# Meta keys of four attention items in one transpose, index dot products on two row halves, one triangle for the forget sums

## What is computed

```python
# A: forgetting attention, 8 heads of 64
log_f = log_sigmoid(fa + b_forget)
log_f_cum = cumsum(log_f, axis=1)                        # forget sums, (tokens, 8)
s = q @ k.T * scale + f_q - f_k; p = softmax(masked s); o = p @ v
# B: sparse attention, 8 heads; an indexer of 4 heads of 64 picks 64 keys for each query
dots   = einsum('bqhd,bkd->bhqk', q_idx, k_idx)          # 4 index heads, one set of index keys
iscore = einsum('bqh,bhqk->bqk', idx_w, relu(dots)) * 64 ** -0.5
top_score, top_idx = top_k(iscore, 64)
# attention over the chosen keys, then the two branches gated, merged and projected
# mixture of experts: for each expert rows @ w_gate_up[e], clamped SwiGLU, @ w_down[e]
```

## Time and profile before

| | |
|---|---|
| median of 3 runs | 1165.92 us (1164.47 to 4083.46) |
| profiled execution | 1165.41 us, its span 1163.6 us |
| granted PE clock, mean | 0.989 of full speed |
| busy share | PE 95%, PE weight loads 45%, DVE 29%, ACT 18%, POOL 1% |
| DMA | 433.66 MB, mean 373 GB/s |

### The profile page before, as it was taken

One profiled execution on the slowest core, in us unless ns is written; L12 is line 12 of the kernel. 1 busy time (PEld: TensorE's weight loads), 2 busy tenths in 40 slices (PEclk: granted clock), 3 DMA queues, 4 the chain that ended last, 5 costly groups with the idle time before them and its releaser, 6 DMA issues. The chain is left out here.

```text
span 1163.6 us, 13610 instructions
## 1 busy us (share of the span) xinstructions
PE 1101.5 (95%) x5490; PEld 526.2 (45%) x5490; DVE 332.2 (29%) x774; ACT 203.7 (18%) x359; POOL 14.2 (1%) x27
## 2 busy tenths in 40 slices
PE   8999999999999989898989998989999999899997
PEld 6878888554343434343434343433333333343433
DVE  2256443132323131313131313131313131313223
ACT  2438781031101010101010101010101010101012
POOL 3010000000000000000000000000000000000000
PEclk9999999999999999999989999999999999999999
DMA  9814237869999999999999999999999999999994
GB/s 309 278 36 128 90 110 291 359 223 423 422 433 431 431 433 430 431 433 430 433 431 432 431 432 430 433 431 431 433 430 433 430 431 433 431 431 431 426 426 164
DMA packets 39750, 433.66 MB, mean 373 GB/s; under 512 B 3160, under 2 KB 19698, under 8 KB 23204
## 3 DMA queue, kind: packets, MB, share of 16 engines
q1 hardware_dynamic: 38160, 429.45, 88.1%
q0 software_dynamic: 960, 2.30, 0.6%
q10 hardware_dynamic: 596, 1.45, 0.4%
HBM read 432.13 MB, written 1.05 MB: 372 GB/s over the span
## 5 line engine op out<-in xcount | busy, mean ns | idle before, releaser
L1738 PE MATMUL psum<-arena 128*64 128x512 f32 x1016 | 224.4, 595 | 11.0 <-DMA arena<-in_w_gate_up 10.9
L1738 PE MATMUL psum<-ring,arena 128*64 128x512 f32 x968 | 217.4, 604 | 9.2 <-DMA ring<-in_w_gate_up 9.2
L1738 PEld LDWEIGHTS psum<-arena 128*64 128x64 f32 x1016 | 70.9, 137 | 156.8 <-issue 139.9
L1754 PE MATMUL psum<-ring,arena 128*64 128x512 f32 x544 | 123.7, 608 | 15.5 <-DMA ring<-in_w_down 9.1
L1738 PEld LDWEIGHTS psum<-ring,arena 128*64 128x64 f32 x968 | 68.2, 139 | 151.1 <-issue 148.8
L1196 DVE TENSOR_TENSOR arena<-psum,biasT 128x512 f32<-128x512 f32 x64 | 44.3, 692 | 292.3 <-PE psum L1710 288.0
L859 DVE TENSOR_TENSOR arena<-psum,vT 128x512 f32<-128x512 f32 (+1 forms) x42 | 28.4, 681 | 341.7 <-PE psum L1637 331.8
L1754 PE MATMUL psum<-arena 128*64 128x512 f32 x480 | 108.0, 603 | 10.4 <-DMA arena<-in_w_down 10.4
L773 ACT ACTIVATE arena<-psum 128x1024 f32<-128x1024 f32 x32 | 32.7, 1023 | 325.1 <-PE psum L1738 311.7
L1754 PEld LDWEIGHTS psum<-ring,arena 128*64 128x64 f32 x544 | 42.2, 140 | 85.5 <-issue 85.5
L1220 DVE TENSOR_TENSOR h<-h,psum 128x1024 f32<-128x1024 f32 x64 | 75.3, 1218 | 16.0 <-PE psum L1779 14.0
(11 more groups left out here) (233 smaller groups left out, 762.2 us busy)
## 6 DMA issues: line engine op xcount, KB each, us to landing
arena<-in_w_gate_up SPq DMA_DIRECT2D x28, 4096.0 KB, 30.2
ring<-in_w_gate_up SPq DMA_DIRECT2D x27, 4096.0 KB, 30.0
arena<-in_w_down SPq DMA_DIRECT2D x14, 4096.0 KB, 30.1
ring<-in_w_down SPq DMA_DIRECT2D x12, 4096.0 KB, 30.1
ring<-in_w_in SPq DMA_DIRECT2D x14, 1024.0 KB, 12.5
arena<-in_w_gate_up SPq DMA_DIRECT2D x13, 1024.0 KB, 15.9
arena<-in_w_gate_up SPq DMA_DIRECT2D x5, 2048.0 KB, 25.2
ring<-in_w_down SPq DMA_DIRECT2D x10, 1024.0 KB, 16.4
```

Of the source, the lines that this page charges most:

```text
L1738: ins = mm(bank[home + n][h * CAP:(h + 1) * CAP, :], xg[:, c, e * CAP:(e + 1) * CAP], w[:, h * D + n * 512:h * D + (n + 1) * 512], start=c ...
L1754: ins = mm(bank[1][n * CAP:(n + 1) * CAP, :], act[:, c * CAP:(c + 1) * CAP], w[:, n * 512:(n + 1) * 512], start=first, stop=last)
```

## The change

Three edits, all in the mixer:

- **Forget sums.** `ltri` is a strict triangle; the sum had one product with `ltri` and one with the identity for each tile. Now DVE adds the two matrices once (`tri`, in a buffer that is free until the attention loop), and each tile has one product. PE waits for `s_tri`.
- **Index heads.** Two heads' index queries (2 x 64 columns) are transposed together, so that odd heads land in rows 64 to 127. The index keys are copied into both halves of the rows (two DVE copies, `s_kiT`). The products of heads h and h + 1 are issued one after the other on different row halves, into different banks.
- **Meta keys.** DVE writes the 16 meta columns of item k, multiplied, into columns 32 (k % 4) of a buffer `prm` (two halves of 128 columns), with an instruction of its own, then the remaining columns as before. For every fourth item PE transposes the 128 columns of `prm` at once into the bank of that item, and DVE copies the four strips out, ahead of the item's own copy. The other three items have no meta transpose and no meta copy.

```diff
-        qiT = late[:, 0:IH * SEQ].rearrange("p (h k) -> p h k", h=IH)
+        qiT = late[:, 0:IH * SEQ // 2].rearrange("p (h k) -> p h k", h=IH // 2)
...
-        pT = take(4 * 384)
+        pT = take(2 * 640)
+        prm = take(2 * P)
...
+        tri = pT[0][:, 0:P]
...
-                copy_out(("qiT", t), qiT[0:ID, :, t * P:(t + 1) * P],
-                         job_bank(("qiT", t))[0:ID, :].rearrange("p (h k) -> p h k", h=IH))
+                copy_out(("qiT", t), qiT[:, :, t * P:(t + 1) * P],
+                         job_bank(("qiT", t))[:, 0:IH // 2 * P].rearrange("p (h k) -> p h k", h=IH // 2))
...
             dve.wait_ge(s_kst, 16)
+            v.tensor_tensor(tri, ltri, ident, ALU.add).then_inc(s_tri, 1)
...
-            v.tensor_copy(kiT[0:ID, :], job_bank(("kkT", 0))[0:ID, 0:KEYS])
+            for n in range(2):
+                v.tensor_copy(kiT[n * ID:(n + 1) * ID, :], job_bank(("kkT", 0))[0:ID, 0:KEYS]).then_inc(s_kiT, 1)
...
-                    v.tensor_scalar(pr[:, k % 3, 0:w], pr[:, k % 3, 0:w], rk[:, 32 + k:33 + k], None,
+                    heads_meta = slice(k % 8 * 32, k % 8 * 32 + META)
+                    v.tensor_scalar(prm[:, heads_meta], pr[:, k % 3, 0:META], rk[:, 32 + k:33 + k], None, ALU.mult)
+                    v.tensor_scalar(pr[:, k % 3, META:w], pr[:, k % 3, META:w], rk[:, 32 + k:33 + k], None,
                                     ALU.mult).then_inc(s_pn, 1)
...
-                    v.tensor_copy(dst[0:META, 384 + t * P:384 + (t + 1) * P], src[0:META, 256:384])
+                    if k % 4 == 3:
+                        for m in range(4):
+                            v.tensor_copy(pT[2 * (pair % 2) + m // 2][0:META, 384 + m % 2 * P:384 + (m % 2 + 1) * P],
+                                          src[32 * m:32 * m + META, 256:384])
                     empty_end(v.tensor_copy(dst[:, t * P:t * P + (t + 1) * P], src[:, 0:(t + 1) * P]), ("PT", k))
...
             pe.wait_ge(s_logf, 1)
+            pe.wait_ge(s_tri, 1)
...
-                terms = [(lf[0:rows, t, :], ltri[0:rows, 0:rows]), (lf[0:rows, t, :], ident[0:rows, 0:rows])]
+                terms = [(lf[0:rows, t, :], tri[0:rows, 0:rows])]
...
-                for h in range(IH):
-                    ins = tr(job_bank(name)[0:ID, h * P:(h + 1) * P],
-                             qtok[:, t, 768 + h * ID:768 + (h + 1) * ID], ident)
+                for h in range(IH // 2):
+                    ins = tr(job_bank(name)[:, h * P:(h + 1) * P],
+                             qtok[:, t, 768 + 2 * h * ID:768 + 2 * (h + 1) * ID], ident)
                 fill_end(ins, name)
+            pe.wait_ge(s_kiT, 2)
             wait_emptied(pe, ("kkT", 0))
...
-                for h in range(IH):
-                    name = ("dots", t, h)
-                    fill_begin(pe, name)
-                    fill_end(mm(job_bank(name)[:, 0:WIDTH[t]], qiT[0:ID, h, t * P:(t + 1) * P],
-                                kiT[0:ID, 0:WIDTH[t]], start=True, stop=True), name)
+                for h in range(0, IH, 2):
+                    for u in range(2):
+                        fill_begin(pe, ("dots", t, h + u))
+                    for u in range(2):
+                        name = ("dots", t, h + u)
+                        part = slice(u * ID, (u + 1) * ID)
+                        fill_end(mm(job_bank(name)[:, 0:WIDTH[t]], qiT[part, h // 2, t * P:(t + 1) * P],
+                                    kiT[part, 0:WIDTH[t]], start=True, stop=True), name)
...
-                    tr(job_bank(name)[:, k * P:(k + 1) * P], pr[:, i % 3, META + k * P:META + (k + 1) * P],
-                       ident)
-                fill_end(tr(job_bank(name)[0:META, 256:384], pr[:, i % 3, 0:META], ident), name)
+                    ins = tr(job_bank(name)[:, k * P:(k + 1) * P],
+                             pr[:, i % 3, META + k * P:META + (k + 1) * P], ident)
+                if i % 4 == 3:
+                    ins = tr(job_bank(name)[:, 256:384], prm[:, i // 4 % 2 * P:(i // 4 % 2 + 1) * P], ident)
+                fill_end(ins, name)
```

More of the change, by code:

```diff
@@ L320, in build @@
         s_nf = sem("forget_row_beside_keys")
+        s_tri = sem("inclusive_triangle_ready")
+        s_kiT = sem("index_keys_in_both_halves")
         s_kk = sem("index_and_rope_keys_ready")
```

## The result

| | before | after |
|---|---|---|
| median | 1164.88 us (18 runs, 1163.60 to 1166.12 but for one of 4083.46) | 1167.62 us (18 runs, 1166.10 to 1169.01) |
| ratio | | 1.0021, 95% interval 1.0014 to 1.0027 |
| profiled execution, its span | 1165.41, 1163.6 us | 1167.12, 1165.3 us |

The account below looks back on a forecast made before the run. PE bounds the front up to the first expert load at 184.55 us, DMA the rest. Terms -0.49 - 0.20 + 0.135 - 1.4 = -1.95 us took 1165.41 to 1163.5 us; range 1160.7 to 1166.6 us.

Parts of the forecast that it names:

- What bounds the kernel: Whole kernel: PE-bound front of 251 us, DMA-bound rest of 906 us; time off PE's way to 184.55 us moves the end equally.
- Part 1: Forget sums: one triangle removes 6 of 18 PE passes, 0.49 us less on PE.
- Part 2: Index queries and dot products: 0.20 us less from ACT's shorter copy; faster dot products count zero, covered by DVE's selection.
- The term for ACT's copy: Index queries, first tile: ACT's copy takes 0.38 us instead of 0.58, so 0.20 us go.
- The fourth rival: Index dot products: the two row halves run in series, still 1163.5 us; counted within the forecast's 0.55.
- Part 3, the saving: Attention loop: 32 meta transposes become 8, 2.6 us less on PE; about 0.1 us lost at the last transpose.
- Part 3, the multiplication: Second DVE multiplication by 1/sum, 16 meta columns: +0.135 us per item, on the path at the first item.
- Part 3, the copies: End of each four items: four meta copies at 0.20 us steps, +0.60; values 0.14 us late, seven places costing 1.14 us.
- My own sign of being wrong: Values in the attention loop: the prediction is wrong if they wait for over 0.4 us.
- the three other places: Three of the loop's seven waits before the values: slack 0.655 us instead of 0.71, so 0.195 us late each.
- the third: End of each four items: DVE's burst becomes the bound, 0.73 us at each of seven places, 1167.4 us; chance 0.15.

Follow-up runs that it names:

- e6: e3 with the index heads as in the kernel before, one head per transpose and products one by one: 1161.70 us, ratio 0.9977 to the kernel before.
- e7: e3 with six rounds of DVE's selection instead of eight for each tile, so 48 keys picked instead of 64: 1160.48 us, one run.
- e8: e6 with six rounds of DVE's selection instead of eight for each tile, so 48 keys picked instead of 64: 1160.10 us, one run.
- e3: Changed kernel, but the fourth item's main copy comes first with its own signal, the four meta strips after it: 1163.14 us, ratio 0.9981 to the kernel before.
- e4: Changed kernel with all four strip copies reading rows 0 to 15, which alters the attention's meta part: 1164.58 us, ratio 0.9997 to the kernel before.
- e5: Changed kernel with ACT's copies of finished pairs of heads two loop steps later: 1167.07 us, ratio 1.0013 to the kernel before.
- e2: Kernel before with the meta-key part alone: 1167.50 us, ratio 1.0020 to the kernel before.
- e9: Kernel before with the index part alone, two heads on two row halves: 1164.65 us, ratio 0.9993 to the kernel before.
- e10: Kernel before with the forget part alone, one triangle for the sums: 1164.55 us, ratio 0.9997 to the kernel before.
- e11: e3 with the second tile's selection spread over the attention loop's DVE steps: 1159.54 us, ratio 0.9950 to the kernel before.
- e1: Changed kernel with meta keys handled as before, so forget and index parts only: 1164.20 us, ratio 0.9991 to the kernel before.
- e12: e6 with the second tile's selection spread over the attention loop's DVE steps: 1161.42 us, ratio 0.9967 to the kernel before.

## Why the prediction was wrong, step by step

- **What bounds the kernel**: right. PE's way to the first expert load sets the end; the last stage kept its length and rate. By profiles, the change's own terms sum to +2.07 us at the first load (-0.49 forget sums, -0.09 index queries, +0.13 first multiplication, +2.52 loop). That lies inside the 1.6 to 3.1 us of the measurement. The sum had -1.95, so it missed by 4.0.
- **Part 1**: right. -0.49 forecast, 2.19 to 1.70 us measured. Its rows after, as the earlier trace rows:

```profile
56.68 0.52 PE L1447 MATMUL psum<-arena 16*8 16x16 f32 x4
...
58.38 4.13 PE L1456 MATMUL psum<-arena 128*128 128x512 f32 x9
```

- **Part 2**: right that the dot products give nothing behind DVE's selection, and the cover was named rightly (e6, e7, e8). PE waits 1.58 us at its first transpose where I had said some 1.9. What covers them is DVE's selection, which reads no PSUM, so the rule on emptying PSUM that I had cited isn't what acts here. The term for ACT's copy was too large: from the first transposes of the queries (74.09 us) to the first product it is 1.28 us, against 1.37, so 0.09 went and not 0.20. The copy itself is 0.20 shorter (0.38 us), but the product starts 0.21 us after its end, where it was 0.10; why, no run shows. The fourth rival is false: 16 passes from 75.37 to 77.16 us, 1.79 where they took 2.98, so float32 products on two row halves do run together. Its rows, as the earlier trace rows:

```profile
74.09 0.60 PE L1485 MATMUL psum<-kst,arena 128*128 128x128 f32 x4
...
75.37 1.86 PE L1498 MATMUL psum<-arena 64*128 64x144 f32 x16 [0.68 <-issue]
...
77.16 1.13 PE L1475 MATMUL psum<-ring,arena 128*128 128x256 f32 x4
```

- **Part 3, the saving**: right but for its end. 24 passes of 0.109 us are 2.62; e3 shows 2.27 of it. From one set of values to the next it takes 10.63 us where it took 10.96, that is 0.33 for three passes. But from the seventh to the eighth it takes 10.02, against 10.04: the last four transposes need 0.79 us (176.29 to 177.08) where five needed 0.59, 0.16 of it idle until the last multiplication is done. So the loss at the end is 0.35 us and not 0.1.
- **Part 3, the multiplication**: right, +0.13 us on the path at the first item.
- **Part 3, the copies**: the step of the prediction that failed is "four meta copies stand there instead of one, at a step of 0.20 us: +0.60". The 0.20 was read from one meta copy between instructions that start in the same rows. Reading four strips from four sets of rows costs 0.30 a step (e4 sets them back to 0.20 and the wait to my 0.14). That makes this part of the burst 0.985 us longer, not 0.60. The values start 0.57 us late at the four plain places, not 0.14. My own sign of being wrong, a wait of over 0.4 us, is there.
- The second failure stands in the same paragraph: for the three other places I took 0.655 us of slack without asking why it was not 0.71. The 0.05 was ACT's copy, already late. In the shorter pattern the exponential holds 1/sum up by 0.27 us, and the delay there is 0.84 (e5 takes the 0.27 away). Four times 0.57 and three times 0.84 are 4.8 us where the sum has 1.14. That difference, 3.7 us, is the bulk of the miss of 4.0; the end of the loop gives 0.25 and ACT's copy of the queries 0.1 more.
- **Rivals**: the third, DVE's burst as the bound, is what happened, down to its 1167.4 us and its limit of 0.45 us at each place. But its parts were wrong: copies at their full length, yes, but PE's restart was 0.12 and not 0.38, the small multiplication overlapped, and ACT, which I had not seen, supplied the difference. So its total was right partly by luck (5.1 us for the seven places against 4.8). I gave it 0.15 because overlapping starts were what the rows that I had picked showed; the pair with L961 I had not read for this. The step of the copies had no bound of its own in the range: at 0.30 us it puts 7 x 0.4 = 2.8 us on top. The end of the range, 1166.6, doesn't follow from its terms either (1164.8 + 1.5 is 1166.3); the result lies above both.

What stays open is a term that may not be the change's. In the stretch from the first load to the first refill the profiled run of after takes 67.47 us, before it was 66.59. Windows of one microsecond in it, columns as above:

```profile
246.00:247.00 1.00, 0.63 (x4) 0.52 (x4) 0.20 (x2) 0.98 (x2) 0.00 (x0) 1.00 1.07 459
247.00:248.00 1.00, 0.39 (x2) 0.39 (x3) 0.86 (x5) 0.99 (x3) 0.00 (x0) 0.78 0.83 291
248.00:249.00 1.00, 1.00 (x6) 1.00 (x6) 0.28 (x3) 0.23 (x2) 0.00 (x0) 0.50 1.03 262
...
251.00:252.00 1.00, 1.00 (x6) 0.40 (x7) 0.71 (x3) 0.00 (x0) 0.00 (x0) 1.00 0.00 0
```

PE is busy for only 1.02 of 2 us here, and then gets 1.2 GHz in place of 2.4 for 3.4 us. But the kernel before has the same gap and keeps 1.00:

```profile
244.55:245.55 1.00, 0.59 (x6) 0.40 (x5) 0.47 (x5) 0.98 (x2) 0.00 (x0) 1.00 0.77 328
245.55:246.55 1.00, 0.32 (x4) 0.20 (x3) 0.58 (x3) 1.00 (x1) 0.00 (x0) 1.00 0.88 369
```

So do e2, e4, e6, e8, e9, e10 and e11 with the same shares. The fall is in 6 of the 14 profiled kernels: in five of the eight with the row halves (after, e1, e3, e5, e7; not e4, e9, e11) and in one of the six without (e12). It costs 0.9 to 1.5 us where it comes (67.5 to 68.1 us against 66.6). One profile of each kernel can't say what tips it, or whether it comes more often in some kernels, and so not whether a part of the change's loss is due to it.

## What to carry to other kernels

When work is gathered into one burst, put what the next engine waits for first in it and give it a signal of its own; here the same copies, reordered, turned 2.5 us lost into 2.2 won. Measure the step of queued instructions on the pattern that will run: a step read between instructions on the same rows doesn't hold for ones that change rows. Before booking a gain on PE, look for the in-order chain of another engine that its next reader stands behind, and shorten or spread that chain first.

## What the hardware showed that I had not expected

- 16x128 float32 copies from PSUM by VectorE, issued in a row, start 0.20 us apart when all read from the same rows, and 0.286 to 0.305 us apart when each reads from another set of 32 rows, with 0.272 to 0.292 us for one. So they stop overlapping.
- Float32 products with 64 rows on the two halves of the rows run together: 16 passes in 1.79 us against 2.98 in series. These times still hold the waits for free banks.
- TensorE's weight load starts 0.12 us after the copy that releases it (139.90 to 140.02), after 0.69 us of idle time, and by the same 0.12 us at all seven places of the loop.
